# Second norm of a hybrid decoder layer: where the squares of the output projection's results are made

## The reference

```
def rmsnorm(x, g):
    r = lax.rsqrt(jnp.mean(xf * xf, axis=-1, keepdims=True) + EPS)
    return xf * r * g

x = x + (sigmoid(ga) * y_a + sigmoid(gb) * y_b) @ w_o      # output projection and residual
xn = rmsnorm(x, g2)                                        # the second norm
up = xn @ w_up                                             # 1024 -> 5632
... causal convolution of width 3, silu(a) * gval, @ w_down, residual, last norm
```

## Time and profile before

| | |
|---|---|
| median of 3 runs | 900.88 us (900.83 to 901.25) |
| the profiled execution | 900.66 us, of which the span of the profile is 898.8 us |
| TensorE busy | 890.2 us, 99% of the span |
| VectorE, ScalarE, GpSimd busy | 66%, 43%, 15% |
| output projection, on TensorE | from 466.0 us to 512.2 us |

### The profile page before, as it was taken

How to read it: one execution, slowest core, us unless ns; L and a number is a source line. 1 busy time by engine, 2 the same in 40 slices (tenths; PEclk the granted TensorE clock), 3 DMA queues, 4 the chain that set the end, 5 groups by cost and what they waited for, 6 DMA issues and landing times.

```text
span 898.8 us, 19220 instructions
## 1 busy us (share of the span) xinstructions
PE 890.2 (99%) x7330; PEld 885.9 (99%) x7330; DVE 595.8 (66%) x946; ACT 386.0 (43%) x613; POOL 134.9 (15%) x182
## 2 busy tenths in 40 slices
PE   8999999999999999999999999999999999999997
PEld 8999999999999999999999999999999999999997
DVE  7895774443884445677755677777777778966544
ACT  7545434534863323344433344444444444433334
POOL 0673000002541111000005800000000000000001
PEclk9999999999999999999999999999999999999999
DMA  6332253234872222322355222222222222333232
GB/s 213 114 123 94 71 205 101 72 102 156 285 277 77 72 70 70 97 90 94 96 179 137 91 93 93 93 93 93 86 84 89 92 93 88 98 107 87 90 106 96
DMA packets 31495, 100.37 MB, mean 112 GB/s; under 512 B 4668, under 2 KB 7260, under 8 KB 31192
## 3 DMA queue, kind: packets, MB, share of 16 engines
q1 hardware_dynamic: 29256, 92.96, 31.5%
q0 software_dynamic: 1472, 5.72, 2.1%
q10 hardware_dynamic: 720, 1.04, 0.4%
HBM read 92.37 MB, written 7.35 MB: 111 GB/s over the span
## 4 chain that ended last, share of the span: by engine, by line
PE 91%; POOLq 3%; issue 3%; DMA 1%; POOL 1%; ACT 0%; SPq 0%; ACTq 0%
PE out L1924 84%; PE trp L1924 3%; PE aux L1924 2%; POOLq L1902 2%; POOLq L1900 1%; PE trp L1956 1%; DMA cwb<-in_conv_wb 1%; DMA raw_pair<-in_w_slots 1%; PE aux L2113 0%; POOL y L1915 0%; POOL out_conv_old L1886 0%; ACT xg L579 0%; POOLq L1893 0%; POOLq L87 0%; POOL sconv L1894 0%
## 5 line engine op out<-in xcount | busy, mean ns | idle before, releaser
L579 ACT ACTIVATE whi<-raw_pair 128x1024 fp32r<-128x1024 f32 (+3 forms) x164 | 154.5, 947 | 227.4 <-PE out L1924 213.6
L1068 DVE TENSOR_TENSOR wlo<-raw_pair,whi 128x1024 fp32r<-128x1024 f32 (+1 forms) x127 | 162.6, 1280 | 131.0 <-ACT whi L579 130.6
L1924 PE MATMUL out<-xh,whi 128*128 128x260 f32 x708 | 149.5, 288 | 0.0
L1924 PE MATMUL out<-xh,wlo 128*128 128x260 f32 x708 | 145.5, 283 | 0.0
L1924 PE MATMUL out<-xl,whi 128*128 128x260 f32 x708 | 145.4, 283 | 0.0
L1924 PE MATMUL out<-x2h,wlo 128*128 128x260 f32 x704 | 142.0, 283 | 0.0
L1924 PE MATMUL out<-x2h,whi 128*128 128x260 f32 x704 | 141.9, 283 | 0.0
L1924 PE MATMUL out<-x2l,whi 128*128 128x260 f32 x704 | 141.7, 283 | 0.0
L1924 PEld LDWEIGHTS out<-xh,whi 128*128 128x128 f32 x708 | 110.8, 189 | 0.5
L1924 PEld LDWEIGHTS out<-xh,wlo 128*128 128x128 f32 x708 | 110.3, 188 | 0.0
L1924 PEld LDWEIGHTS out<-xl,whi 128*128 128x128 f32 x708 | 110.2, 188 | 0.0
(11 more groups left out here) (362 smaller groups left out, 1683.0 us busy)
## 6 DMA issues: line engine op xcount, KB each, us to landing
raw_pair<-in_w_slots SPq DMA_DIRECT2D x123, 512.0 KB, 3.3
raw_pair<-in_w_dn SPq DMA_DIRECT2D x16, 448.0 KB, 3.3
c_ring<-in_C_state SPq DMA_DIRECT2D x8, 512.0 KB, 5.5
row<-scratch SPq DMA_DIRECT2D x8, 512.0 KB, 6.1
out_C_sample<-c_ring SPq DMA_DIRECT2D x8, 512.0 KB, 5.0
raw_pair<-in_w_dn SPq DMA_DIRECT2D x8, 512.0 KB, 3.5
xres<-in_x_all POOLq DMA_DIRECT2D x1, 1560.0 KB, 6.7
x<-in_x_all SPq DMA_DIRECT2D x5, 260.0 KB, 6.7
```

The lines of the kernel that those rows point to most:

```text
L579: return act.activation(out, in_, func, **kw_)
L1068: TT(wlo[p][:, 0:width], raw[p][:, 0:width], whi[p][:, 0:width].bitcast(F32), ALU.subtract)\
L1924: return pe.matmul(*a, **k)
```

## The change

ScalarE makes the squares, behind x2h[j] in its loop, into ftmp[j mod 2]. GpSimd only adds them up. Two semaphores are new: s_x1q counts squares made; s_x1a counts buffers free: GpSimd gives it 2 before its loop and 1 with each addition, and ScalarE waits for j + 1 of it ahead of square j. The nop that gives the 2 stands behind the memset of acc and its drain.

```
@@ scalar, output projection
                     A(x2h[:, i * 2 + t, :], x1[:, i * 2 + t, :], scale=gains[:, 2, bass.ds(i * 2 + t, 1)]).then_inc(s_x2h, 1)
+                    apart()
+                    act.wait_ge(s_x1a, i * 2 + (t + 1))
+                    A(ftmp[t][:, :], x1[:, i * 2 + t, :], ACT.Square).then_inc(s_x1q, 1)
@@ gpsimd
             pool.memset(acc[:, :], 0.0)
             pool.drain()
+            pool.nop().then_inc(s_x1a, 2)
             for j in range(KT):
-                pool.wait_ge(s_x1, j + 1)
-                pool.tensor_tensor(sqa[:, :], x1[:, j, :], x1[:, j, :], ALU.mult)
-                pool.drain()
-                pool.tensor_tensor(acc[:, :], acc[:, :], sqa[:, :], ALU.add)
+                pool.wait_ge(s_x1q, j + 1)
+                pool.tensor_tensor(acc[:, :], acc[:, :], ftmp[j % 2][:, :], ALU.add).then_inc(s_x1a, 1)
                 pool.drain()
             pool.nop().then_inc(s_acc, 1)
```

More of the change, by code:

```diff
@@ L423, in hybrid_layer @@
         s_acc = sem("norm2_sums")
+        s_x1q = sem("x1_squared")
+        s_x1a = sem("x1_squares_summed")
         s_ss2 = sem("norm2_broadcast")
```

## The result

The changed kernel takes 909.79 us (median of 4 runs, 909.31 to 910.6) against 900.97 us before: a ratio of 1.0098, with a 95% interval of 1.0086 to 1.011. It is 8.8 us slower. The forecast was 910.9 us, which is 10.25 us above the profiled execution of before (900.66). The profiled execution has a span of 907.6 us, 8.8 us above the span of before.

The account below looks back on a forecast made before the run. TensorE, busy for 99% of the span, was taken to bound the kernel. Gap 8.65, clock 1.5 and last sum 0.1 us made 10.25 us on the profiled execution's 900.66: 910.9 us, range 907.0 to 913.5.

Parts of the forecast that it names:

- the other two terms: Lower clock after TensorE's gap, 1.5 us, and a later last sum at the end of the output projection, 0.1 us.
- signs of being wrong: TensorE's gap under 4 us, clock staying at 1.00 through it, or a second gap of a microsecond later in the stage.
- Who bounds the stage, and what can be won: Output projection, 465 to 540 us: TensorE bounds it; a faster norm can win at most 0.28 us.
- The wait and its queue: ScalarE stands still from 473.9 until GpSimd's nop, holding back the split, low part and TensorE tile of S_WO + 3.
- The gap: TensorE idle from 483.4 to 492.05, before the tile of S_WO + 3: 8.65 us, bounds 4.6 and 9.6.
- the nop: GpSimd's nop behind its preparation, passed at 489.06 before: 0.4 us taken off, 488.65, so ScalarE's square starts at 488.7.
- The rest of the restart: After the nop: square 0.62 us, split 1.06, VectorE's low part 1.55, TensorE 0.1 later, at 492.05.
- The first rival: GpSimd's preparation, released by a quiet VectorE, brings the nop up to 3.7 us earlier: 907.2 us; chance 0.12.
- The clock: Matmuls after TensorE's gap start at 1.2 GHz; three microseconds at half speed lose 1.5 us, bounds 0.5 and 3.4.
- The last sum: End of the stage: the last square waits for ScalarE's x2h, so GpSimd's sum ends later: +0.1 us, between -0.28 and +0.4.
- Square under the table in force: Rival: Square isn't in Sigmoid's table, so loads of 1.28 us come with ScalarE's squares: 912.2 us; chance 0.08.

Follow-up runs that it names:

- Experiment 1: Changed kernel with free buffers given ahead of GpSimd's preparation: 900.67 us; kernel before with only ScalarE's wait added, squares left on GpSimd: 910.31 us.
- experiment 5: Changed kernel plus ten VectorE operations, SBUF inputs 909.77 us, PSUM 909.69; plus an unread 512 KB load 911.73; buffers given early, S_WO + 5 load held: 900.93.

## Why the prediction was right

The place, the cause and the size held; of the sum, the gap was put 1.5 us too long, and the other two terms came within 0.2 us. The forecast time lies only 1.1 us above the median, as it was built on an execution 0.3 us below the median of before. None of the signs of being wrong appeared; ScalarE's idleness (13.4 us for some 15) and TensorE's gap (7.1 for 8 to 9) were shorter than announced.

- **Who bounds the stage, and what can be won**: right. With the buffers given early, the median is 0.2 us below that of before, with an interval that includes no change.
- **The wait and its queue**: right in every link. ScalarE stood from 473.9 to 487.4; the split, the low part and the tile of S_WO + 3 followed in the order forecast. Experiment 1 shows that the wait is enough.
- **The gap**: 8.65 us forecast, 7.1 measured, within the bounds of 4.6 and 9.6. The step that was mis-sized is the nop. The square was put at 488.7 and came at 487.37. The drain was 2.1 us shorter than I took it to be, and the addition into sconv 0.5 shorter (0.4 forecast); against that, the constants for the convolution landed 0.95 us later in this execution. I kept the drain at its length of before because I asked only whether VectorE's silence would shorten it. It doesn't (experiment 5). I had listed the load of S_WO + 5 among what the wait holds back, and asked only whether it would come late itself, not whom its absence would serve. The rest of the restart, from square to matmul, took 3.22 us against 3.35.
- **The first rival** (GpSimd released by a quiet VectorE) put the drain up to 3.7 us shorter. It was 2.1 us shorter, but not by that mechanism: experiment 5 shows VectorE busy and the drain as short.
- **The clock**: 1.5 us forecast, 1.65 measured, by the same reasoning of three-odd microseconds at half speed. The other half of the reasoning doesn't carry over. The prediction read from the kernel's end that 1 to 2 us of idleness were enough; there the clock fell 1.3 us after the last matmul (893.81 to about 895.1), but TensorE had been busy for only 0.44 to 0.81 of each microsecond from 891 to 894. In this stage it had worked without a pause. With a gap of 1.5 us the clock stayed at 1.00, and in the six profiles with a longer gap it fell 3.5 to 4.7 us after the last matmul ahead of it. The gap was long enough for either reading. The rows of the kernel before:

```profile
892.00:893.00 1.00, 0.44 (x5) 0.36 (x5) 0.17 (x1) 0.64 (x2) 0.00 (x0) 1.00 1.04 356
893.00:894.00 1.00, 0.81 (x8) 0.63 (x6) 0.59 (x2) 0.15 (x1) 0.00 (x0) 1.00 1.00 357
894.00:895.00 1.00, 0.00 (x0) 0.00 (x0) 1.00 (x5) 0.22 (x1) 0.70 (x2) 1.00 0.31 98
```

- **The last sum**: +0.1 forecast, slightly below zero measured. It was there 4.15 us behind the start of ScalarE's last split (523.66 + 1.72, against 521.23), and before after 4.25 (516.72 against 512.47). The sum started 0.28 us later by that measure, and this was made good by the addition, which took 1.72 us beside VectorE and not the 2.10 of before.
- **Square under the table in force**: no load came with it. The one load of the stage still stands ahead of Sqrt, and was free as forecast.
- **Two slips in the working** change nothing in the forecast. A projection tile is 48 matmuls, or 24 pairs of 0.24 us, and not 48 pairs. And "2.3 us" for two additions and a memset doesn't lead from 479.53 to 482.2: the 3.07 us from 485.99 to 489.06 less 0.4 do, 2.67 us.

The gap is 7.11 us (483.48 to 490.59), and the tile was due 0.04 us later than before. With the 1.65 us behind the restart, which hold the clock's price and the little that the last sum gave back, this makes 8.8 us, the difference between the spans and between the medians.

## What to carry to other kernels

A wait added to an engine that works in order must be asked two things: when is it first met, and what stands behind it in that engine's program that others need. Here a buffer that had been free all along was declared free at the end of an unrelated preparation, and the notice, not the buffer, cost 1% of the kernel; the same notice given ahead of that preparation cost nothing. When a stall is priced, also list what it holds back besides the critical work: here a load that didn't run shortened a store by 2 us, and with it the very wait that was being priced.

## What the runs showed of the hardware

- A gap in TensorE's work costs more than its length, and the extra doesn't grow with the gap: 1.55 to 2.2 us for gaps from 4.7 to 8.1 us, which is half of the 3.3 to 4.6 us worked at a granted clock of 0.50 behind the restart. After a gap of 1.5 us it was 0.1 us, with the granted clock at 1.00 throughout. These figures are of one profiled execution of each kernel; others were up to 2 us longer at a lower mean clock.
- GpSimd's drain behind the issue of a store in short runs (176 KB, of 32 bytes each) lasts 4.4 us, and 6.3 to 6.5 us when a load of 512 KB from SyncE's queue runs beside it (5.1 us where the product ahead of the drain was itself a microsecond longer). Ten VectorE operations beside it change nothing, whether with two inputs in SBUF or one in PSUM. Whether GpSimd waits for room among the transfers still outstanding or for something else wasn't tried.
- Even with no store issued shortly before, the drain behind the first two products took 1.3 us, in both runs that moved the store.
